# The triangular inverse of an RWKV-7 head kernel: from 128x128 blocks on the whole array to 64x64 blocks in two opposite corners of it

## The chip, the cores and the metric

One core of one Trainium2 chip runs the whole program. The metric is the device time of one execution in microseconds (us). Everything is fp32, or fp32 split into a high and a low part.

## The reference, cut to what matters

Two transformer-like blocks run one after the other on a sequence of 256 tokens of width 1024. The first has an SSD mixer, an attention and a mixture of experts. The second has an RWKV-7 mixer, a convolution and a feed-forward layer. The change touches only the recurrence of the RWKV-7 mixer, which the reference writes token by token for 16 heads of 64 values:

```
sa = einsum('bhvk,bhk->bhv', S, -kk_t)
S  = S * w_t + sa[..., None] * (kk_t * a_t) + v_t[..., None] * k_t
o_t = einsum('bhvk,bhk->bhv', S, r_t)
```

The kernel computes it by blocks of 128 tokens. Within a block the values `sa` depend on each other through a strictly lower triangular 128x128 matrix L, one for each head and token block, and the kernel needs the inverse of I + L. After that, everything is plain products.

## The kernel before, in words

The heads go in 8 pairs (`PAIRS`). A pair has 4 units, 2 heads by 2 blocks of 128 tokens, and `unit(h, t)` numbers them. One step of the loop over pairs interleaves two things on each engine: the inverse of pair p, and the rest of the pair before (`tail`) together with the preparation of the next (`prep`). The order is written out by hand, one function `step` for each engine, in `pe_heads`, `act_heads` and `dve_heads`. Engines hand over by semaphores, and every engine takes its instructions in the written order. Step 0 has no tail, step 7 has no preparation, and `step_loop` runs steps 1 to 6 as a hardware loop of two steps on PE and ACT (DVE writes its own).

The inverse runs by doubling. At level `lev`, `XT` holds the transposed inverses of all diagonal blocks of 2^lev rows and `Xm` the same not transposed. There are seven levels (`LEV`), up to blocks of 128. A level has three parts:

- `below` (line 2269): for each unit, the product of L with the inverse so far, 128x128 by 128x128. The four calls go to two PSUM banks, two units each; such a pair of units is a group g.
- `mask` (L2609, DVE): one instruction for each group keeps the identity and the blocks just under the diagonal, and writes `Ym` (`Xm` at level 0).
- `grow`: for each unit, one product that gives the new half of `Xm` (L2283, not at the last level) and one that gives the new half of `XT` (L2287). Only the 64 columns that change are streamed, picked by the strided view `halves`. ACT copies them back, `Xm` first (L2453) and then `XT` (L2454), one instruction for each group.

Between these, PE works off the tail: `rest` (L2296, L2299), `solve` (L2307), `state` (L2313, L2314) and `outputs` (L2326 to L2328); and the preparation: `decays` (L2224), `turn_ar` and `turn_bk` (transposes) and `grams` (L2252). `grams` contracts over 64 rows only; its calls alternate between the upper and the lower half of the array's rows and write to two different banks.

On DVE, `mask_grams` (L2590) masks the four gram matrices of the next pair. After the second of each two it turns L into I - L (L2599) and writes the level-0 `XT` (L2602). The first half of this stands ahead of the mask of level 6, the second half behind it. The rest of DVE's work of a step, in pieces between the masks, is `differences`, `key_direction`, `state`, `key_and_bonus`, `make_ar`, `make_bk` and `centre` (L2555 to L2630).

In the trace each call of a matmul in fp32 shows as two weight loads and two matmuls; a transpose shows as one of each.

Of the kernel before, what the change touches and what calls it, by code (L numbers as in the profile page):

```python
# [61 lines left out]
def constants():  # L62
# [16 lines left out]
    for lev in range(7):  # L79
        m = 1 << lev  # L80
        pick = ((i[:, None] // m) % 2 == 1) & (i[None, :] // m == i[:, None] // m - 1)
        put(f"level{lev}", np.eye(P) + pick)
        if lev == 0:
            put("level0_t", np.eye(P) + pick.T)
# [100 lines left out]
def build(nc, A, out):  # L185
    ctx = ExitStack()
    with ctx:
# [1982 lines left out]
        Xm, Ym = carve(8960, 4, P), carve(9472, 4, P)  # L2170
# [47 lines left out]
        def pe_heads(pe):  # L2218
# [39 lines left out]
            def below(p, b, lev):  # L2258

                for g in range(2):  # L2260
                    if lev == 0:
                        pe.wait_ge(inverse_begun, 2 * p + g + 1)
                    elif lev == 1:
                        pe.wait_ge(*y_masked.at(2 * LEV * p + g + 1))
                    else:
                        pe.wait_ge(*xm_copied.at(2 * (LEV - 2) * p + 2 * lev + g - 3))
                    for v in range(2):
                        u = 2 * g + v
                        mm = nc.tensor.matmul(bank[g][:, v * P:(v + 1) * P], gram[b][:, u, 0:P],  # L2269
                                              ident if lev == 0 else Xm[:, u, :], start=True, stop=True)  # L2270
                    mm.then_inc(y_made, 1)

            def grow(p, b, lev):

                even, odd = halves(Ym, lev)[0], halves(XT[b], lev)[1]
                for g in range(2):
                    pe.wait_ge(*y_masked.at(2 * LEV * p + 2 * lev + g + 1))
                    if not (isinstance(p, int) and p == 0 and lev == 1):
                        pe.wait_ge(xt_copied, 2 * (LEV - 1) * p + 2 * lev + g - 3)
# [23 lines left out]
            def solve(p, c, t):  # L2303
                pe.wait_ge(xt_copied, 2 * (LEV - 1) * (p + 1))
# [96 lines left out]
            def last():  # L2401
# [16 lines left out]
                pe.wait_ge(xt_copied, 2 * (LEV - 1) * PAIRS)  # L2418
# [7 lines left out]
            step_loop(pe, first, step, last)  # L2426

        def act_heads(act):
# [18 lines left out]
            def grown(p, b, lev):  # L2447
                for g in range(2):
                    r = slice(2 * g, 2 * g + 2)
                    new = bank[2 + g][:, 0:2 * P].rearrange("p (a u n m) -> p a u n m", a=2, u=2, m=1 << lev)  # L2450
                    act.wait_ge(x_made, 2 * (LEV - 1) * p + 2 * lev + g - 1)
                    if lev < LEV - 1:
                        nc.scalar.copy(halves(Xm[:, r, :], lev)[0], new[:, 0]).then_inc(xm_copied.sem, 1)  # L2453
                    nc.scalar.copy(halves(XT[b][:, r, :], lev)[1], new[:, 1]).then_inc(xt_copied, 1)  # L2454
# [9 lines left out]
            def step(p, b, tail=True, prep=True):  # L2464
# [22 lines left out]
                grown(p, b, 5)  # L2487
                grown(p, b, 6)
# [53 lines left out]
        def dve_heads(dve, order):  # L2542
# [44 lines left out]
            def mask_grams(p, c, units):  # L2587
                for u in units:
# [5 lines left out]
                    if u % 2:  # L2594

                        g = slice(u - 1, u + 1)
                        dve.wait_ge(*gram_masked.at(4 * p + u + 1))
                        lt = gram[c][:, g, 0:P]
                        order.step(nc.vector.scalar_tensor_tensor(out=lt, in0=lt, scalar=-1.0,  # L2599
                                                                  in1=ident.unsqueeze(1).to_broadcast([P, 2, P]),  # L2600
                                                                  op0=ALU.mult, op1=ALU.add))
                        nc.vector.tensor_tensor(XT[c][:, g, :], lt, con("level0_t").unsqueeze(1).to_broadcast([P, 2, P]),  # L2602
                                                ALU.mult).then_inc(inverse_begun, 1)

            def mask(p, lev):

                for g in range(2):
                    dve.wait_ge(y_made, 2 * LEV * p + 2 * lev + g + 1)
                    nc.vector.tensor_tensor((Xm if lev == 0 else Ym)[:, 2 * g:2 * g + 2, :],  # L2609
                                            bank[g][:, 0:2 * P].rearrange("p (u s) -> p u s", u=2),  # L2610
                                            con(f"level{lev}").unsqueeze(1).to_broadcast([P, 2, P]),
                                            ALU.mult).then_inc(y_masked.sem, 1)
# [21 lines left out]
            def step(p, b, tail=True, prep=True):  # L2634
# [30 lines left out]
                if prep:  # L2665
                    mask_grams(p + 1, c, (2, 3))

# [31 lines left out]
            def first():  # L2699
                dve.wait_ge(*c_low.at(4))  # L2700
                dve.wait_ge(rk_loaded, 32)
# [8 lines left out]
                mask_grams(0, 0, (2, 3))  # L2710
                gate_convolution(1)
# [288 lines left out]
```

## Time and profile before

| | us |
|---|---|
| median of 3 runs | 1545.48 |
| lowest, highest | 1539.59, 1552.73 |
| profiled execution: its own time | 1549.11 |
| profiled execution: span of the trace | 1547.3 |
| PE busy over the span | 1386.0 (90%) |
| weight loads | 1130.7 (73%) |
| DVE busy | 861.6 (56%) |
| ACT busy | 718.1 (46%) |
| POOL busy | 608.3 (39%) |

PE is TensorE's matmuls, PEld its weight loads, DVE is VectorE, ACT is ScalarE, POOL is GpSimd. A matmul's recorded time is the time it takes to go through the array, and several are under way at once, so a busy share near 100% of PE does not say that it is at its peak; how fast it works is read from the distances between the starts. The page counts the mean granted clock of TensorE over the whole span as 0.938 of full speed. The loop over head pairs occupies the time from about 1064 to 1266 us, in which almost no data is loaded.

### The profile page before, as it was taken

To read this page: it belongs to the slowest core of one execution; us is meant where nothing else is said; L and a number is where in the kernel's file an instruction comes from. 1 tells how busy PE (TensorE), PEld (TensorE's weight loads), DVE (VectorE), ACT (ScalarE), POOL (GpSimd) and SP (SyncE) were. 2 spreads that over 40 slices of the span, in tenths; PEclk is the share of its full clock that TensorE was granted. 3 is DMA by queue.
4 is the path that set the end of the run, shared out by engine and by line. 5 is a ranking of instruction groups with operands and counts; after the bars stand their busy time and mean duration, and the time that the engine had idled before them with its cause. 6 is when DMAs were issued, how large, how long until landed. Compare 5 with 4: busy or idle time off the path is not lost.

```text
span 1547.3 us, 20663 instructions
## 1 busy us (share of the span) xinstructions
PE 1386.0 (90%) x6880; PEld 1130.7 (73%) x6880; DVE 861.6 (56%) x1436; ACT 718.1 (46%) x1209; POOL 608.3 (39%) x324
## 2 busy tenths in 40 slices
PE   5989998788899999997599998859999998799996
PEld 4877876676677777775477776647999986678885
DVE  2283253435688888886413999975666654211112
ACT  4455464434475757665443334443333323344442
POOL 5858658440000000001666565613000005478784
PEclk9989998699999999999899998969999999799999
DMA  6647443038399999993465364612000004355562
GB/s 205 174 118 194 136 134 109 1 109 267 112 354 323 319 310 315 320 317 106 122 196 162 109 190 130 184 42 69 1 0 0 0 11 167 109 163 176 176 190 82
DMA packets 127255, 239.93 MB, mean 155 GB/s; under 512 B 16296, under 2 KB 32346, under 8 KB 127056
## 3 DMA queue, kind: packets, MB, share of 16 engines
q1 hardware_dynamic: 116384, 227.12, 45.9%
q10 hardware_dynamic: 10801, 11.89, 2.7%
q8 instruction: 41, 0.67, 0.2%
q14 instruction: 29, 0.24, 0.0%
HBM read 234.79 MB, written 1.05 MB: 152 GB/s over the span
## 4 chain that ended last, share of the span: by engine, by line
PE 42%; issue 39%; POOL 9%; DVE 7%; ACT 2%; DMA 1%; POOLq 0%; DVEq 0%; ACTq 0%
POOL wlo L291 9%; PE bank L297 7%; PE bank L298 6%; PE bank L299 6%; PE bank L2269 3%; PE bank L2287 3%; PE bank L2283 2%; PE bank L2784 2%; PE bank L2786 2%; PE bank L2785 2%; DVE work L764 2%; PE bank L369 1%; PE bank L2252 1%; DVE work L457 1%; DVE work L998 1%
## 5 line engine op out<-in xcount | busy, mean ns | idle before, releaser
L291 POOL TENSOR_TENSOR wlo<-raw,whi 128x1024 fp32r<-128x1024 f32 (+1 forms) x232 | 565.0, 2454 | 713.8 <-ACT whi L286 713.3
L297 PE MATMUL bank<-whi,t0h 128*128 128x512 f32 (+1 forms) x1072 | 443.1, 413 | 22.0 <-POOL wlo L291 6.7
L286 ACT ACTIVATE whi<-raw 128x1024 fp32r<-128x1024 f32 (+1 forms) x300 | 309.3, 1053 | 280.8 <-PE bank L299 237.7
L298 PE MATMUL bank<-wlo,t0h 128*128 128x512 f32 (+1 forms) x1072 | 431.3, 402 | 0.0
L299 PE MATMUL bank<-whi,t0l 128*128 128x512 f32 (+1 forms) x1072 | 430.9, 402 | 0.0
L297 PEld LDWEIGHTS bank<-whi,t0h 128*128 128x128 f32 x1072 | 208.8, 195 | 79.0 <-issue 23.2
L299 PEld LDWEIGHTS bank<-whi,t0l 128*128 128x128 f32 x1072 | 207.6, 194 | 49.1
L298 PEld LDWEIGHTS bank<-wlo,t0h 128*128 128x128 f32 x1072 | 208.2, 194 | 46.0 <-issue 1.7
L291 DVE TENSOR_TENSOR wlo<-work,whi 128x1024 fp32r<-128x1024 f32 x96 | 113.0, 1218 | 7.5 <-ACT whi L286 7.4
L286 ACT ACTIVATE whi<-work 128x1024 fp32r<-128x1024 f32 x96 | 97.9, 1054 | 5.1 <-PE bank L1459 5.1
L369 PE MATMUL bank<-const,work 128*128 128x128 f32 x128 | 28.8, 419 | 66.4 <-DVE work L457 55.2
L291 DVE TENSOR_TENSOR wlo<-raw,whi 128x1024 fp32r<-128x1024 f32 x68 | 80.2, 1219 | 14.1 <-ACT whi L286 14.1
L2050 DVE SCALAR_TENSOR_TENSOR bank<-work,proj,bank 128x256 f32<-128x256 f32 x203 | 84.8, 483 | 1.9
L2527 POOL TENSOR_TENSOR proj<-proj,small x8 | 5.9, 734 | 194.5 <-PE bank L2328 194.5
L2609 DVE TENSOR_TENSOR work<-bank,const 128x256 f32<-128x256 f32 x112 | 46.6, 423 | 58.3 <-PE bank L2269 54.5
L369 PEld LDWEIGHTS bank<-const,work 128*128 128x128 f32 x128 | 26.1, 226 | 69.5 <-DVE work L457 41.0
L2899 DVE TENSOR_TENSOR t1l<-bank,t1h 128x512 fp32r<-128x512 f32 x16 | 10.3, 686 | 112.3 <-ACT t1h L2856 112.3
L2453 ACT COPY work<-bank 128x128 f32<-128x128 f32 x80 | 21.4, 267 | 82.1 <-PE bank L2287 82.1
L2287 PE MATMUL bank<-work 128*128 128x64 f32 x384 | 57.6, 276 | 1.9 <-DVE work L2609 1.9
L1457 PE MATMUL bank<-whi,t1h 128*128 128x512 f32 x128 | 53.5, 418 | 2.9 <-DVE wlo L291 2.8
L2269 PE MATMUL bank<-work 128*128 128x128 f32 x384 | 55.6, 287 | 0.4 <-DVE work L2609 0.4
L2287 PEld LDWEIGHTS bank<-work 128*128 128x128 f32 x384 | 49.9, 192 | 4.8 <-issue 3.5
(413 smaller groups left out, 2030.0 us busy)
## 6 DMA issues: line engine op xcount, KB each, us to landing
raw<-in_w_ff SPq DMA_DIRECT2D x64, 512.0 KB, 3.6
raw<-in_w_in SPq DMA_DIRECT2D x60, 496.0 KB, 3.6
raw<-in_w_in SPq DMA_DIRECT2D x56, 512.0 KB, 3.6
work<-in_w_exp_down SPq DMA_DIRECT2D x68, 256.0 KB, 5.0
work<-in_w_exp_gate SPq DMA_DIRECT2D x62, 256.0 KB, 5.2
work<-in_w_exp_up SPq DMA_DIRECT2D x62, 256.0 KB, 6.2
raw<-in_w_exp_down SPq DMA_DIRECT2D x60, 256.0 KB, 4.7
raw<-in_w_exp_gate SPq DMA_DIRECT2D x34, 256.0 KB, 5.3
```

Source lines behind the costliest of these rows:

```text
L286: nc.scalar.activation(whi[:, s, 0:width], raw_of(n)[:, 0:width], ACT.Copy).then_inc(hi_ready, 1)
L291: ins = (nc.vector if split_by_vector(n) else nc.gpsimd).tensor_tensor(wlo[:, s, 0:width], raw_of(n)[:, 0:width], whi[:, s, 0:width].bitca ...
L297: nc.tensor.matmul(dst, hi, wh, start=first, stop=False)
L298: nc.tensor.matmul(dst, hi, wl, start=False, stop=False)
L299: return nc.tensor.matmul(dst, lo, wh, start=False, stop=last)
L369: tr = nc.tensor.transpose(bank[4 + b][:, at:at + P], self.src[:, t, (2 * b + kk) * P:(2 * b + kk + 1) * P], ident)
L764: ins = nc.vector.scalar_tensor_tensor(out=convT[:, c, :], in0=xbcT[:, c, w:w + SEQ], scalar=tap, in1=convT[:, c, :], op0=ALU.mult, op1=AL ...
L1457: nc.tensor.matmul(bank[4 + h][:, :], hh, whi[:, s, f], start=first, stop=False, skip_group_check=True)
L2050: ins = nc.vector.scalar_tensor_tensor(out=cvT[:, c, :] if w == W2 - 1 else partial(c), in0=uT[:, c, w:w + SEQ], scalar=tap, in1=partial(c ...
L2269: mm = nc.tensor.matmul(bank[g][:, v * P:(v + 1) * P], gram[b][:, u, 0:P], ident if lev == 0 else Xm[:, u, :], start=True, stop=True)
L2287: mm = nc.tensor.matmul(bank[2 + g][:, P + v * 64:P + (v + 1) * 64], Ym[:, u, :], odd[:, u], start=True, stop=True)
L2609: nc.vector.tensor_tensor((Xm if lev == 0 else Ym)[:, 2 * g:2 * g + 2, :], bank[g][:, 0:2 * P].rearrange("p (u s) -> p u s", u=2), con(f"l ...
```

## The change

- The inverse is made first for the two 64x64 diagonal blocks of each unit, packed above each other: rows 0 to 63 of `XD`, `Xm` and `Ym` belong to the upper block, rows 64 to 127 to the lower. Every product of levels 0 to 5 becomes two calls with 64 rows and 64 columns, one in the upper left corner of the array and one in the lower right, which write to different partitions of the same PSUM bank.
- The growth products stream all 64 columns of a block, and `halves` picks the new ones when ACT copies them.
- Level 6 joins the two blocks: the lower left part of L times the upper inverse (no mask, a plain copy), and that times the lower inverse. ACT copies the two finished diagonal blocks from `XD` into `XT` (`diagonal`), and the quarter of `XT` that stays zero is cleared once at the start.
- `begin_inverse` is taken out of `mask_grams` and stands behind the mask of level 6 and the last gram masks.
- PE's steps 1 to 6 are written out rather than looped. The counts of the semaphores follow.

```diff
-    for lev in range(7):
+    i64 = np.arange(64)
+    for lev in range(6):
...
-        put(f"level{lev}", np.eye(P) + pick)
+        put(f"level{lev}", np.tile(np.eye(64) + pick, (2, 1)))
...
-        Xm, Ym = carve(8960, 4, P), carve(9472, 4, P)
+        Xm, Ym = carve(8960, 4, 64), carve(9472, 4, 64)
+        XD = [carve(9216 + 512 * c, 4, 64) for c in range(2)]
+        XT_COPIES = 2 * (LEV - 1) + 2
+        HALF = [slice(64 * a, 64 * a + 64) for a in range(2)]
...
                     for v in range(2):
                         u = 2 * g + v
-                        mm = nc.tensor.matmul(bank[g][:, v * P:(v + 1) * P], gram[b][:, u, 0:P],
-                                              ident if lev == 0 else Xm[:, u, :], start=True, stop=True)
+                        o = bank[g][:, v * 64:(v + 1) * 64]
+                        if lev == LEV - 1:
+                            mm = nc.tensor.matmul(o[HALF[1]], gram[b][HALF[0], u, 64:P], Xm[HALF[0], u, :], start=True,
+                                                  stop=True)
+                            continue
+                        for r in HALF:
+                            mm = nc.tensor.matmul(o[r], gram[b][r, u, r], ident[r, r] if lev == 0 else Xm[r, u, :],
+                                                  start=True, stop=True)
                     mm.then_inc(y_made, 1)
...
                     if lev < LEV - 1:
                         for v in range(2):
                             u = 2 * g + v
-                            nc.tensor.matmul(bank[2 + g][:, v * 64:(v + 1) * 64], XT[b][:, u, :], even[:, u], start=True,
-                                             stop=True)
-                    for v in range(2):
-                        u = 2 * g + v
-                        mm = nc.tensor.matmul(bank[2 + g][:, P + v * 64:P + (v + 1) * 64], Ym[:, u, :], odd[:, u],
-                                              start=True, stop=True)
+                            for r in HALF:
+                                nc.tensor.matmul(bank[2 + g][r, v * 64:(v + 1) * 64], XD[b][r, u, :], Ym[r, u, :], start=True,
+                                                 stop=True)
+                        for v in range(2):
+                            u = 2 * g + v
+                            for r in HALF:
+                                mm = nc.tensor.matmul(bank[2 + g][r, P + v * 64:P + (v + 1) * 64], Ym[r, u, :],
+                                                      XD[b][r, u, :], start=True, stop=True)
+                    else:
+                        for v in range(2):
+                            u = 2 * g + v
+                            mm = nc.tensor.matmul(bank[2 + g][HALF[0], v * 64:(v + 1) * 64], Ym[HALF[1], u, :],
+                                                  XD[b][HALF[1], u, :], start=True, stop=True)
...
-            step_loop(pe, first, step, last)
+            first()
+            for p in range(1, PAIRS - 1):
+                step(p, p % 2)
+            last()
...
+                        nc.scalar.copy(halves(Xm[:, r, :], lev)[0], halves(new[:, 0], lev)[0]).then_inc(xm_copied.sem, 1)
+                        nc.scalar.copy(halves(XD[b][:, r, :], lev)[1], halves(new[:, 1], lev)[1]).then_inc(xt_copied, 1)
+                    else:
+                        nc.scalar.copy(XT[b][HALF[0], r, 64:P],
+                                       bank[2 + g][HALF[0], 0:P].rearrange("p (u s) -> p u s", u=2)).then_inc(xt_copied, 1)
+
+            def diagonal(p, b):
+                act.wait_ge(xt_copied, XT_COPIES * p + 2 * (LEV - 2))
+                for r in HALF:
+                    nc.scalar.copy(XT[b][r, :, r], XD[b][r, :, :]).then_inc(xt_copied, 1)
...
                 grown(p, b, 5)
+                diagonal(p, b)
                 grown(p, b, 6)
...
+            def begin_inverse(p, c):
+                for u in (1, 3):
...
+                    order.step(nc.vector.scalar_tensor_tensor(out=lt, in0=lt, scalar=-1.0,
+                                                              in1=ident.unsqueeze(1).to_broadcast([P, 2, P]),
+                                                              op0=ALU.mult, op1=ALU.add))
+                    for r in HALF:
+                        nc.vector.tensor_tensor(XD[c][r, g, :], gram[c][r, g, r],
+                                                con("level0_t")[r].unsqueeze(1).to_broadcast([64, 2, 64]),
                                                 ALU.mult).then_inc(inverse_begun, 1)
...
+                    y = bank[g][:, 0:P].rearrange("p (u s) -> p u s", u=2)
+                    if lev == LEV - 1:
+                        ins = nc.vector.tensor_copy(Ym[HALF[1], 2 * g:2 * g + 2, :], y[HALF[1]])
+                    else:
+                        ins = nc.vector.tensor_tensor((Xm if lev == 0 else Ym)[:, 2 * g:2 * g + 2, :], y,
+                                                      con(f"level{lev}").unsqueeze(1).to_broadcast([P, 2, 64]), ALU.mult)
...
                 mask(p, 6)
                 if prep:
                     mask_grams(p + 1, c, (2, 3))
+                    begin_inverse(p + 1, c)
...
             def first():
                 dve.wait_ge(*c_low.at(4))
+                for c in range(2):
+                    order.mark(nc.vector.memset(XT[c][HALF[1], :, 0:64], 0.0))
```

## Rows read from the trace of the kernel before

**Rows 1.** Busy time by stretch: length, each engine's busy time, granted clock, DMA share, GB/s.

```profile
core 0: us, PE busy (x) PEld busy (x) DVE busy (x) ACT busy (x) POOL busy (x), PEclk, DMA share, GB/s
1060.00:1260.00 200.00, 193.95 (x1610) 180.82 (x1609) 127.61 (x306) 62.11 (x237) 14.58 (x16) 1.00 0.01 3
1106.60:1132.20 25.60, 25.09 (x213) 23.64 (x212) 16.75 (x41) 8.00 (x31) 1.43 (x2) 1.00 0.01 2
```

**Rows 2.** Groups by line and shape, 1060 to 1270 us: busy, mean ns, idle before.

```profile
L2287 PE MATMUL bank<-work 128*128 128x64 f32 x384 | 57.6, 276 | 1.9 <-DVE work L2609 1.9
L2269 PE MATMUL bank<-work 128*128 128x128 f32 x384 | 55.6, 287 | 0.4 <-DVE work L2609 0.4
...
L2609 DVE TENSOR_TENSOR work<-bank,const 128x256 f32<-128x256 f32 x112 | 46.6, 423 | 58.3 <-PE bank L2269 54.5 <-DMA raw<-in_ln_x_b 1.6
...
L2453 ACT COPY work<-bank 128x128 f32<-128x128 f32 x80 | 21.4, 267 | 82.1 <-PE bank L2287 82.1
```

**Rows 3.** Timeline of one level inside a step: start, duration, engine, line.

```profile
1119.12 0.53 PEld L2283 LDWEIGHTS bank<-work 128*128 128x128 f32 x4
...
1119.57 0.53 PEld L2287 LDWEIGHTS bank<-work 128*128 128x128 f32 x4
...
1120.52 0.61 PE L2287 MATMUL bank<-work 128*128 128x64 f32 x4
...
1121.16 0.27 ACT L2453 COPY work<-bank 128x128 f32<-128x128 f32 x1 [0.46 <-PE bank L2287]
...
1121.58 0.97 PEld L2269 LDWEIGHTS bank<-work 128*128 128x128 f32 x8
1121.63 1.11 PE L2269 MATMUL bank<-work 128*128 128x128 f32 x8
...
1122.33 0.87 DVE L2609 TENSOR_TENSOR work<-bank,const 128x256 f32<-128x256 f32 x2 [1.47 <-PE bank L2269]
1122.47 0.53 PEld L2307 LDWEIGHTS bank<-work 128*128 128x128 f32 x4
```

**Rows 4.** Timeline of the end of that step, from the last growth to the next level 0.

```profile
1131.68 0.53 PEld L2287 LDWEIGHTS bank<-work 128*128 128x128 f32 x4
...
1132.27 0.73 PEld L2252 LDWEIGHTS bank<-work 64*128 64x128 f32 x8
1132.28 1.13 PE L2252 MATMUL bank<-work 64*128 64x256 f32 x8
...
1133.34 0.97 PEld L2269 LDWEIGHTS bank<-work 128*128 128x128 f32 x8 [0.33 <-issue]
...
1133.44 1.29 DVE L2590 TENSOR_TENSOR work<-bank,const 128x512 f32<-128x512 f32 x2 [0.66 <-PE bank L2252]
1134.76 0.42 DVE L2599 SCALAR_TENSOR_TENSOR work<-work,const 128x256 f32<-128x256 f32 x1
1134.78 0.73 PEld L2252 LDWEIGHTS bank<-work 64*128 64x128 f32 x8 [0.47 <-DVE work L2590]
...
1135.56 0.75 DVE L2609 TENSOR_TENSOR work<-bank,const 128x256 f32<-128x256 f32 x2
...
1137.54 0.42 DVE L2599 SCALAR_TENSOR_TENSOR work<-work,const 128x256 f32<-128x256 f32 x1
...
1138.00 0.42 DVE L2602 TENSOR_TENSOR work<-work,const 128x256 f32<-128x256 f32 x1
...
1138.85 0.87 DVE L2609 TENSOR_TENSOR work<-bank,const 128x256 f32<-128x256 f32 x2 [0.43 <-PE bank L2269]
```

**Rows 5.** Timeline, the same place one step later.

```profile
1157.92 0.49 PE L2252 MATMUL bank<-work 64*128 64x256 f32 x2
```

**Rows 6.** Weight loads by shape, whole trace.

```profile
L2283 PEld LDWEIGHTS bank<-work 128*128 128x128 f32 x320 | 42.2, 192 | 1.3 <-DVE work L2609 0.7 <-issue 0.5
...
L1891 PEld LDWEIGHTS bank<-proj,work 128*64 128x64 f32 x32 | 4.3, 137 | 2.7 <-issue 0.4
```

**Rows 7.** DVE and ACT instructions of other sizes, 1060 to 1270 us.

```profile
L2590 DVE TENSOR_TENSOR work<-bank,const 128x512 f32<-128x512 f32 x28 | 17.9, 682 | 6.7 <-PE bank L2252 6.7
...
L2441 ACT COPY work<-bank 128x512 f32<-128x512 f32 x7 | 4.1, 586 | 0.1
...
L2432 ACT ACTIVATE work<-bank 128x256 f32<-128x256 f32 x7 | 2.7, 383 | 6.6 <-PE bank L2224 6.6
```

**Rows 8.** Busy time by stretch, in the attention, where the clock was low.

```profile
254.50:268.00 13.50, 11.79 (x57) 10.43 (x57) 4.22 (x14) 5.39 (x18) 10.21 (x25) 0.51 0.06 23
```

More of the change, by code:

```diff
@@ L78, in constants @@
     put("amask", np.concatenate([neg, np.zeros((P, P)), neg], axis=1))
[L79 removed]
+    i64 = np.arange(64)
+    for lev in range(6):
         m = 1 << lev
[L81 to L82 removed]
+        pick = ((i64[:, None] // m) % 2 == 1) & (i64[None, :] // m == i64[:, None] // m - 1)
+        put(f"level{lev}", np.tile(np.eye(64) + pick, (2, 1)))
         if lev == 0:
[L84 removed]
+            put("level0_t", np.tile(np.eye(64) + pick.T, (2, 1)))
     put("heads", (i[:, None] // 64 == i[None, :] // 64) * 1.0)
@@ L2449, in grown @@
                     r = slice(2 * g, 2 * g + 2)
-                    new = bank[2 + g][:, 0:2 * P].rearrange("p (a u n m) -> p a u n m", a=2, u=2, m=1 << lev)
                     act.wait_ge(x_made, 2 * (LEV - 1) * p + 2 * lev + g - 1)
                     if lev < LEV - 1:
-                        nc.scalar.copy(halves(Xm[:, r, :], lev)[0], new[:, 0]).then_inc(xm_copied.sem, 1)
-                    nc.scalar.copy(halves(XT[b][:, r, :], lev)[1], new[:, 1]).then_inc(xt_copied, 1)
+                        new = bank[2 + g][:, 0:2 * P].rearrange("p (a u s) -> p a u s", a=2, u=2)
+                        nc.scalar.copy(halves(Xm[:, r, :], lev)[0], halves(new[:, 0], lev)[0]).then_inc(xm_copied.sem, 1)
[7 more added lines that the diff above has]
+                    nc.scalar.copy(XT[b][r, :, r], XD[b][r, :, :]).then_inc(xt_copied, 1)
             def copy_rest(p, t):
@@ L2593, in mask_grams @@
                                                 [P, 2, 2 * P]), ALU.mult).then_inc(gram_masked.sem, 1)
[L2594 to L2602, printed above, removed]
+            def begin_inverse(p, c):
+                for u in (1, 3):
+                    g = slice(u - 1, u + 1)
+                    dve.wait_ge(*gram_masked.at(4 * p + u + 1))
+                    lt = gram[c][:, g, 0:P]
+                    order.step(nc.vector.scalar_tensor_tensor(out=lt, in0=lt, scalar=-1.0,
[4 more added lines that the diff above has]
+                                                con("level0_t")[r].unsqueeze(1).to_broadcast([64, 2, 64]),
                                                 ALU.mult).then_inc(inverse_begun, 1)
@@ L2608, in mask @@
                     dve.wait_ge(y_made, 2 * LEV * p + 2 * lev + g + 1)
[L2609 to L2612, printed above, removed]
+                    y = bank[g][:, 0:P].rearrange("p (u s) -> p u s", u=2)
[4 more added lines that the diff above has]
+                                                      con(f"level{lev}").unsqueeze(1).to_broadcast([P, 2, 64]), ALU.mult)
+                    ins.then_inc(y_masked.sem, 1)
             def state(p):
@@ L2710, in first @@
                 mask_grams(0, 0, (2, 3))
+                begin_inverse(0, 0)
                 gate_convolution(1)
```

9 lines of the change are left out of this document (4 added, 5 removed).

## The prediction

> **What bounds the kernel now.** I read the busy times by stretch first. Over the loop of head pairs, PE is busy 193.95 of 200 us at full granted clock, DVE 127.61, ACT 62.11, and the DMA share is 0.01 [rows 1]. So no transfer is waited for here, and what the loop saves comes off the total one to one: nothing is loaded in it that could be late behind it. The view of groups by line says who waits for whom. The masks wait 54.5 us for PE's `below`, and the copies of the new half wait 82.1 us for PE's `grow`, while the idle time of PE before the same lines is 1.9 and 0.4 us [rows 2]. PE is the bound and the others wait for it.
>
> The timeline of one level says what PE is bound by. The two calls of L2283 take 0.45 us from their first load to the next line's (1119.12 to 1119.57). The four calls of L2269, with twice as many columns streamed, take 0.89 us (1121.58 to 1122.47) [rows 3]. That is 0.2225 us for a call in both cases, 64 columns or 128: the weight load sets the pace, not the stream. The step repeats after 25.65 us (1132.28 to 1157.92, less 0.01 of rounding) [rows 4, 5]. I split it into the stretch from the first mask of level 0 to the first gram product, 1138.85 to 1157.92 = 19.07 us, and the end of the step, 1132.27 to 1138.85 = 6.58 us [rows 4, 5].
>
> **The change part by part.**
>
> **Cost of a corner call.** A weight load of 64 columns lasts 137 ns where one of 128 lasts 192 [rows 6], 55 ns less, which is half of the 111 ns (0.2225/2) that a load takes up at full pace. The stream of 64 columns needs no more than that. So a corner call takes some 0.0565 us x 2 = 0.113 us; I take 0.116. Do the two corners work at once? The nearest row is L2252: 4 calls of 256 columns each, in the upper and lower row halves by turns, need 1.07 us to the next line's load [rows 4]. At the 0.2225 us for 128 columns of L2269, four calls of 256 columns one after another would take 4 x 0.445 = 1.78 us. So the row halves do run side by side there. I take this for the corners too: 0.116 us for a pair. The bounds are 0.116 (side by side) and 0.232 (in turn) for a pair.
>
> **PE's calls.** Before, a step has 7 x 4 calls of `below` and 5 x 8 + 4 of `grow` = 72, at 0.2225 = 16.0 us. After, there are 6 x 8 + 4 = 52 and 5 x 16 + 4 = 84, 136 in all: 64 pairs and 8 single calls of level 6 = 72 slots at 0.116 = 8.35 us. Gain 7.7 us a step on PE alone.
>
> **Switching.** Before L2252 its load comes 0.59 us after the first load of the four records of L2287, which need 0.445 (1131.68 to 1132.27), so 0.145 us is lost; behind it 1.07 us pass where two pairs need at most 2 x 0.445 = 0.89, so some 0.2 us is lost (0.18 at least), and the load shows 0.33 idle put down to issue [rows 4]. Going between whole-array calls and tiled calls empties the array. The tail and the preparation stay whole-array calls and stand between nearly all parts of the inverse: in at `below` 0, 1, 3, 5 and `grow` 1 to 5, out again as often, 18 new switches a step at 0.145 to 0.2 = 3.1 us. The ends are nothing (if the array stood waiting anyway) and 0.33 each = 5.9 us.
>
> **The long stretch, 19.07 us.** It holds `below` and `grow` 1 to 5, 60 of the calls: 13.35 us become 60 x 0.116 = 6.96, that is -6.4; 16 of the switches add 2.8. PE now also waits where it was covered: behind `below` 0 it needs the mask, behind `grow` the copy of `Xm`, which comes 0.3 us after the last matmul (1120.52 + 0.33 to 1121.16) and takes 0.27, now 64 elements instead of 128, 0.21 by the slope between 128 and 512 elements (267 and 586 ns) [rows 2, 3, 7]. While `grow` of group 1 lasts 0.46 this is 0.1 to 0.2 short at `below` where no filler stands between, hence about 0.3 us over the stretch beside what the switches hide. The sum is -6.4 + 2.8 - 0.3 (the shorter masks) = -3.9: 15.15 us.
>
> **The masks** take 128 elements where they took 256: 424 ns less 128 x 1.0 ns (the slope from 256 to 512 elements, 423 to 682) = 0.30 us [rows 2, 7]; 12 of these and 2 plain copies of the same size. That is 14 x 0.13 = 1.8 us less of DVE's 16.75 us in 25.6 [rows 1]. `begin_inverse` gives 0.35 back (two products of 0.3 for one of 0.42, twice). DVE then has 15.3 us of work; with 0.04 us between neighbours (0.46 from start to start for 0.42, 1137.54 to 1138.00 [rows 4]) for 45 instructions and 1.2 us for one gram product waited for, 18.3: not the bound at 22, but the floor under any better outcome.
>
> **The end of the step, 6.58 us.** Ahead of mask 6 fall the L2599 and L2602 of the first group (0.88 us, 1134.76 to mask 6 at 1135.56, overlapped) [rows 4]. `gram_masked` is unchanged, so the second grams still wait for the first masks: load at +0.05, masks 1.17 us later at the earliest, as 1132.27 to 1133.44; two of 0.65 each; then STT 0.46 and two halves 0.5 until `below` 0 may start, and DVE is busy with the second group for another 0.95 until it takes mask 0. From the first gram product: 1.17 + 1.3 + 1.2 (grams and their latency, with mask 6 inside) + 1.3 + 0.95 + 0.95 = 6.9. The end is 0.3 longer: what moves away ahead of mask 6 is paid at the end, twice over, since `below` 0 of group 0 can no longer begin earlier. `grow` 6, the next `rest` and `decays` lie beside this on PE.
>
> **ACT.** `diagonal` adds two copies of 256 elements, 0.38 each [rows 7]. They stand ahead of the level-6 copies, which wait for mask 6 and the second grams; ACT is 31% busy. I cost them at nothing; if PE's `solve` came to wait for them, 0.77 us a step. The two clears at the start (0.3 each at most, 128x256 masks take 0.42) stand ahead of DVE's first `differences`: 0.7 us at most, which I count. No DMA and no queue of SP or POOL is passed; POOL waits for `outputs` only.
>
> **Sum.** A full step goes from 25.65 to 15.15 + 6.9 = 22.05, -3.6; six of these make -21.6. Step 0, without a tail, has only 4 switches (0.7), but its levels cannot go below the round trip matmul, mask, matmul, copy, about 1.9 us (0.56 + 0.33 + 0.77 + 0.23, from slots, masks and the 0.3 us that a consumer starts late) against 1.39 of calls: 5 levels leave 6.4 - 0.7 - 2.0 = -3.7. Step 7 has 72 calls and the tail's switches, 7.7 - 2.5 - 0.7 = -4.5. With +0.7 for the clears: -29 us. The profiled execution took 1549.1 us, 3.6 above the median of the runs; it goes to 1520, and the median from 1545.5 to 1516.
>
> **The rivals.**
>
> **The corners take turns (slower).** Both corners write to the same PSUM bank, which no pair of row halves in this trace does: `grams` alternates its banks. If the bank admits one of them at a time, the 136 calls cost 136 x 0.116 = 15.8 us, 0.2 less than now, and the switches (3.1) and the end (0.3) come on top: +3.2 us a step, +26 in 8, 1571. The decision lies at 0.165 us a pair: (16.0 - 3.4 - 0.8)/72, with 0.8 for waits. Against it: the corners lie in different partitions, so no output column is shared. The Trainium skill (TensorEngine Tiling, section Gotcha 1: PSUM Pressure) says that different row tiles cannot access the same PSUM bank simultaneously; taken by the letter that is this rival, and no run here shows it yet.
>
> **Dearer switches, or longer waits between levels.** With 0.25 to 0.3 us a switch (the 0.33 above), 18 x 0.1 = 1.8 us more a step: -1.8 x 8 = -14 and 1531. For it: switches into and out of a corner are new, and no row has them.
>
> **The clock falls.** It is granted in full all through the loop, with PE busy 97% [rows 1]. In the attention it stood at 0.51, that is nearly always at 1.2 of 2.4 GHz, with PE busy 11.79 of 13.5 us, at short calls with waits between [rows 8]. After the change PE has 8.35 + 7.9 us of calls in 22 us (7.9 is 25.65 less 16.0 and some 1.7 of waits, 0.47 + 0.33 + 0.43 and smaller ones [rows 4]). If a quarter of the loop ran at half clock, the 16.3 us of calls would last 4 us more in each step and the gain would be gone: 1547.
>
> **More than forecast.** With free switches (-2.8 a step) and waits down to near DVE's floor of 18.3: 19.2 us a step, -6.4 x 8 = -51 and 1494.
>
> **How the numbers follow.** Forecast 0.64 (1498 to 1526), dearer switches 0.13, corners in turn 0.16, the clock 0.04, more than forecast 0.03. The range leaves out most of the corners in turn and a bit below: 1494 to 1562, which holds 0.82. About 1%, or 15 us, is what a measurement of this kernel can tell from no change. Faster by more than that is below 1530: the forecast, the better case, and a little under half of the dearer switches, 0.68 (the forecast's own tail, 0.04, taken off). That tail, the rest of the dearer switches and the clock make 0.16 within 1%, and the corners in turn 0.16 slower.
>
> **What would show it.** Right: the `below` and `grow` groups of two calls a corner start 0.23 and 0.46 us apart from the next; matmuls of the two corners start within some 10 ns of each other; loads near 137 ns; each change to a tail line shows about 0.2 us between matmul and load; the step repeats after some 22 us; masks of 0.3 us; granted clock 1.00. Wrong: corner matmuls at even distances of 0.058 us (in turn), a step above 25.65, masks that no longer wait for PE at all (DVE bound), a PEclk below 0.95 in the loop, or the step's end, first gram to mask 0, much above 6.9.

## The result, and the profile after

| | before | after |
|---|---|---|
| median of 14 runs each, us | 1544.05 | 1531.93 |
| lowest, highest | 1539.59, 1559.53 | 1526.62, 1542.36 |
| profiled execution, its span | 1549.11, 1547.3 | 1526.62, 1524.8 |

The ratio is 0.9923 with a 95% interval of 0.9897 to 0.9950. The kernel is 12 us faster where 29 were forecast; 1531.9 lies inside the stated range of 1494 to 1562. The profiled execution happens to be the fastest of its 14.

The step of the loop repeats from one first gram product (L2256) to the next. These rows of the timeline after (start, duration, engine, line) show three such products, at 1118.75, 1143.86 and 1166.18. Behind the second stands the end of a step, with its second grams (1146.46), up to mask 0 (L2644):

```profile
1118.75 1.14 PE L2256 MATMUL bank<-work 64*128 64x256 f32 x8
...
1143.86 1.13 PE L2256 MATMUL bank<-work 64*128 64x256 f32 x8
...
1146.46 1.13 PE L2256 MATMUL bank<-work 64*128 64x256 f32 x8 [0.86 <-DVE work L2618]
...
1148.80 0.42 DVE L2628 SCALAR_TENSOR_TENSOR work<-work,const 128x256 f32<-128x256 f32 x1
...
1150.35 0.61 DVE L2632 TENSOR_TENSOR work<-work,const 64x128 f32<-64x128 f32 x2
1150.99 0.29 DVE L2644 TENSOR_TENSOR work<-bank,const 128x128 f32<-128x128 f32 x1
1151.01 0.45 PE L2279 MATMUL bank<-const,work 64*64 64x64 f32 x8 [0.65 <-DVE work L2632]
...
1166.18 1.14 PE L2256 MATMUL bank<-work 64*128 64x256 f32 x8
```

The step from 1143.86 takes 22.32 us, 7.13 to mask 0 and 15.19 from there to the next first gram product. Before it was 25.65, 6.58 and 19.07 [rows 4, 5]. But the step before it, 1118.75 to 1143.86, takes 25.11, and the six steps 1 to 6 take 25.14, 22.32, 25.11, 22.32, 23.84 and 23.83 us. The view of busy times by stretch says why. Its columns are those of [rows 1]; the stretches are, by turns, the end of a step (7.1 us) and the rest of it:

```profile
1071.30:1078.40 7.10, 5.23 (x52) 3.87 (x48) 4.99 (x12) 2.45 (x9) 0.00 (x0) 1.00 0.00 0
1078.40:1096.40 18.00, 17.93 (x292) 16.22 (x292) 9.48 (x30) 5.34 (x24) 1.34 (x2) 0.81 0.01 2
1096.40:1103.50 7.10, 5.26 (x52) 3.88 (x48) 5.72 (x14) 2.46 (x10) 0.00 (x0) 1.00 0.01 3
1103.50:1118.70 15.20, 15.09 (x292) 13.52 (x292) 9.45 (x31) 5.32 (x24) 1.34 (x2) 1.00 0.01 2
1118.70:1125.80 7.10, 5.28 (x53) 3.88 (x48) 5.72 (x14) 2.48 (x10) 0.00 (x0) 1.00 0.01 2
1125.80:1143.80 18.00, 17.88 (x292) 16.17 (x292) 9.50 (x31) 5.31 (x24) 1.34 (x2) 0.81 0.01 2
...
1126.60:1133.40 6.80, 6.80 (x79) 6.25 (x77) 3.16 (x11) 1.35 (x6) 0.00 (x0) 0.50 0.00 0
```

Both kinds of step hold the same 292 matmul records in their long part. Where the clock is granted in full they take 15.2 us; where its mean is 0.81, 18.0. In the stretch that begins at 1126.6 it stands at 0.50, at 1.2 of 2.4 GHz. Ahead of each fall lies an end of step in which PE is busy only 5.2 to 5.3 of 7.1 us. The same holds of the ends that no fall follows (5.26 us from 1096.40), so a thin end alone does not decide it. Before the change the clock was 1.00 throughout the loop [rows 1].

The corners themselves work as hoped. These rows of the timeline are `below` 6 (L2275), four calls in one corner; `below` 3 (L2279), eight calls in two corners; `solve` (L2323), two calls on the whole array; and parts of `grow` 3 (L2293, L2298), four calls a line in two corners:

```profile
1144.93 0.67 PE L2275 MATMUL bank<-work 64*64 64x64 f32 x8
...
1157.95 0.68 PE L2279 MATMUL bank<-work 64*64 64x64 f32 x16
1158.56 0.66 PE L2323 MATMUL bank<-work 128*128 128x64 f32 x4
1159.15 0.45 PE L2293 MATMUL bank<-work 64*64 64x64 f32 x8
1159.43 0.40 PE L2298 MATMUL bank<-work 64*64 64x64 f32 x8
1159.66 0.40 PE L2293 MATMUL bank<-work 64*64 64x64 f32 x8
```

Eight calls in two corners take 0.68 us, as four in one do (0.67), and a line of four calls takes 0.23 us (1159.43 to 1159.66): 0.115 us a pair. The rows also price the switches. Eight corner calls need 4 x 0.115 = 0.46 us and `solve` starts 0.61 behind their start, so 0.15 is lost; the two calls of `solve` need 0.445 and the next corner call starts 0.59 behind theirs, so 0.145 is lost. A weight load of a corner lasts 142 ns in the mean, where one of the whole array lasted 192 [rows 6]:

```profile
L2298 PEld LDWEIGHTS bank<-work 64*64 64x64 f32 x640 | 26.7, 142 | 0.0
```

A second loss lies ahead of the loop. In the timeline after, DVE, POOL and PE in the prelude:

```profile
1054.13 2.74 DVE L2632 TENSOR_TENSOR work<-work,const 64x128 f32<-64x128 f32 x2
1054.38 2.34 POOL L292 TENSOR_TENSOR wlo<-raw,whi 128x1024 fp32r<-128x1024 f32 x1 [1.66 <-ACT whi L287]
1056.90 1.29 DVE L2732 TENSOR_TENSOR proj<-proj,bank 128x512 f32<-128x512 f32 x2
1058.24 1.16 PE L2228 MATMUL bank<-proj,const 128*128 128x128 f32 x4 [5.09 <-DVE proj L2732]
```

The last two instructions of `begin_inverse` (L2632), 0.60 or 0.61 us elsewhere, take 2.74 us here. They end at 1056.87, just behind POOL's making of the low part of a weight tile ("POOL's split" below), which is over at 1056.72. The gate of the convolution (L2732) stands behind them on DVE, and PE waits 5.09 us for it. Before the change the same wait was 1.55 us:

```profile
1063.11 0.71 PE L2224 MATMUL bank<-proj,const 128*128 128x128 f32 x4 [1.55 <-DVE proj L2697]
```

The third loss lies behind the loop. These are the stretches from the last first gram product to the first product of the next stage, before and after:

```profile
1234.88:1272.85 37.97, 35.06 (x273) 31.29 (x273) 21.23 (x46) 10.71 (x41) 3.28 (x4) 1.00 0.01 1
1213.85:1253.50 39.65, 33.93 (x404) 28.31 (x401) 20.55 (x50) 11.19 (x45) 3.54 (x4) 0.87 0.01 2
```

This stretch, step 7 and the tail of the last pair, has become 1.7 us longer, with the clock at half for 10.2 us of it.

### The profile page after: what moved, and what is told of

Read it like the earlier page. It is cut to its first block and busy times, and to the rows that moved or that the text cites. A ratio compares the mean times of both kernels' runs of the same rounds, so it can differ in the third digit from the quotient of the medians.

```text
span 1524.8 us, 22521 instructions
## 1 busy us (share of the span) xinstructions
PE 1351.3 (89%) x7904; PEld 1086.8 (71%) x7904; DVE 848.3 (56%) x1454; ACT 717.0 (47%) x1225; POOL 612.0 (40%) x324
## 5 line engine op out<-in xcount | busy, mean ns | idle before, releaser
L292 DVE TENSOR_TENSOR wlo<-raw,whi 128x1024 fp32r<-128x1024 f32 x68 | 80.3, 1221 | 13.9 <-ACT whi L287 13.9
L1458 PE MATMUL bank<-whi,t1h 128*128 128x512 f32 x128 | 53.9, 421 | 2.8 <-DVE wlo L292 2.8
L2644 DVE TENSOR_TENSOR work<-bank,const 128x128 f32<-128x128 f32 x96 | 27.0, 292 | 49.4 <-PE bank L2279 47.8
L2822 PE MATMUL bank<-whi,t1h 128*128 128x512 f32 x128 | 50.7, 396 | 2.1 <-DVE t1l L2937 2.1
L1460 PE MATMUL bank<-whi,t1l 128*128 128x512 f32 x128 | 51.2, 400 | 0.0
L1459 PE MATMUL bank<-wlo,t1h 128*128 128x512 f32 x128 | 51.0, 398 | 0.0
L2824 PE MATMUL bank<-whi,t1l 128*128 128x512 f32 x128 | 50.6, 395 | 0.0
```

Source lines behind the costliest of these rows:

```text
L292: ins = (nc.vector if split_by_vector(n) else nc.gpsimd).tensor_tensor(wlo[:, s, 0:width], raw_of(n)[:, 0:width], whi[:, s, 0:width].bitca ...
L1458: nc.tensor.matmul(bank[4 + h][:, :], hh, whi[:, s, f], start=first, stop=False, skip_group_check=True)
L1459: nc.tensor.matmul(bank[4 + h][:, :], hh, wlo[:, s, f], start=False, stop=False, skip_group_check=True)
L1460: mm = nc.tensor.matmul(bank[4 + h][:, :], hl, whi[:, s, f], start=False, stop=last, skip_group_check=True)
L2822: nc.tensor.matmul(o, t1h[:, c, r], whi[:, s, f], start=False, stop=False, skip_group_check=True)
L2824: mm = nc.tensor.matmul(o, t1l[:, c, r], whi[:, s, f], start=False, stop=last, skip_group_check=True)
```

## The experiments

In what follows, "step" is the time from one first gram product to the next, "prelude" that from the very first one to mask 0 of step 0 (11.30 us before, 15.19 after).

**Filler that keeps PE at work.** Filler is matmul calls whose results are never read: here three small ones a step, put where PE waits for DVE. `busy` is set in steps 1 to 6; the two calls behind `below` 6 stand in step 0 as well, and step 7 has none.

```diff
+            def keep_busy(b, calls, cols=256):
+                for _ in range(calls):
+                    nc.tensor.matmul(bank[b][HALF[1], 256:256 + cols], ident[HALF[1], HALF[1]], con("amask")[HALF[1], 0:cols],
+                                     start=True, stop=True)
...
+                    if busy and g:
+                        keep_busy(1, 1)
...
+                    keep_busy(2, 2)
                     grams(p + 1, c, (2, 3))
```

> The changed kernel, with three calls of filler in each of steps 1 to 6: one corner, 64 rows by 64 columns by 256 streamed, results never read. Two stand where PE waits for the first gram masks (behind `below` 6), one between the two groups of `below` 0, where PE waits for the second half of `begin_inverse`. Theory (the clock): in the changed kernel the loop's steps take 22.32 us while the clock is granted in full and 23.8 to 25.1 us where it is granted in half for 3.4 or 6.8 us, and it falls in the thin stretch from the first grams to level 1. The filler fits into waits of 0.86 and 0.65 us, so it costs at most 0.5 us a step itself. With it the granted clock of the loop is 1.00, all six steps take 22.3 to 22.8 us and the kernel is 6 to 9 us faster than the changed kernel (ratio to before about 0.987). Rival (the long steps are long for another reason, such as instruction fetch of the loop that is written out, and the clock falls because PE waits): the long steps stay at 24 to 25 us with the clock full, and the time is the changed kernel's or up to 3 us more.

All six steps take 22.32 us, 133.91 together against 142.55. The ratio is 0.9877 (0.9849 to 0.9904), the median 1524.42 us, 7.5 less than the changed kernel's. The busy times of the same stretches as above, the six steps as one at the end:

```profile
1092.40:1099.50 7.10, 6.36 (x58) 4.26 (x54) 5.72 (x14) 2.46 (x9) 0.00 (x0) 1.00 0.01 3
1099.50:1114.70 15.20, 15.11 (x292) 13.52 (x292) 9.44 (x31) 5.34 (x24) 1.34 (x2) 1.00 0.01 2
...
1070.09:1204.00 133.91, 128.91 (x2080) 106.67 (x2077) 90.32 (x257) 46.86 (x198) 8.07 (x12) 1.00 0.01 2
```

PE does more work in the end of the step, 6.36 us instead of 5.26, the rest is as it was, and the clock stays at 1.00. The theory holds, and the fetch of the written-out loop, which is still there, is ruled out as the cause of the long steps. In step 7, which has no filler in its `below` 0, the clock falls for 6.8 us where it had fallen for 3.4, and the stretch behind the loop takes 41.07 us instead of 39.65. This fits that of the 8.6 us won in the loop only 7.5 show in the medians.

**The changed kernel again.**

> The changed kernel as it is, beside the combination, so that the two are compared on one chip. Theory (the clock falls by chance of phase, in the thin stretch from the first grams to level 1): the steps again fall into 22.3 us where the clock is full and 23.8 or 25.1 us where it is half for a while, in another pattern than in the first profile; the time is 1528 to 1536 us. Rival (a fixed cause in some steps): the same steps as in the first profile are long.

1532.43 us, ratio 0.9902 (0.9874 to 0.9930). The steps are 25.11, 22.31, 25.10, 22.32, 23.83 and 23.83 us: the same ones are long. So my theory of a chance phase was wrong in this form: the falls came at the same places in both traces of this kernel. The next run shows that the place is not fixed by the step's own code.

**The first inverse begun behind the gate.**

```diff
-                begin_inverse(0, 0)
                 gate_convolution(1)
+                begin_inverse(0, 0)
```

> The changed kernel, with the first inverse begun behind `gate_convolution(1)` in `first` rather than ahead of it. Theory (DVE is held up by POOL in the prelude): in the changed kernel two half instructions of `begin_inverse` take 2.74 us there, until POOL's split of 2.34 us ends, and PE waits 5.1 us for the gate behind them, against 1.55 us before the change. With the gate first, the stretch from the first gram product to mask 0 of step 0 falls from 15.2 to about 12 us and the kernel gains 3 us (ratio to before about 0.990). Rival (the gate itself would then be held up by the same split, or `below` 0 waits for the inverse instead): the stretch stays within 1 us of 15.2 and no time is gained.

The prelude is 13.65 us, a gain of 1.5, half of what was expected. PE now waits 1.38 us for the gate, but the halves meet the next split and last 2.63 us, and `below` 0 waits for them:

```profile
1060.72 2.63 POOL L292 TENSOR_TENSOR wlo<-raw,whi 128x1024 fp32r<-128x1024 f32 x1 [1.67 <-ACT whi L287]
...
1061.18 2.63 DVE L2632 TENSOR_TENSOR work<-work,const 64x128 f32<-64x128 f32 x2
...
1063.87 0.45 PE L2279 MATMUL bank<-const,work 64*64 64x64 f32 x8 [2.29 <-DVE work L2632]
```

So theory and rival were both half right: the gate was held up, and the inverse is held up too. Prelude and step 0 together take 25.65 us instead of 26.34, only 0.7 less; the clock is at half for 3.4 us of this step 0. The loop's code is unchanged here, and yet its long steps are others: 22.31, 25.14, 23.78, 22.31, 25.11 and 22.32 us. So where the falls come depends on what ran ahead of the loop. The ratio, 0.9893 (0.9866 to 0.9920), can't tell 1.5 us.

**The first half of the inverse begun ahead of mask 6 again** (in the loop only).

```diff
                     mask_grams(p + 1, c, (0, 1))
+                    begin_inverse(p + 1, c, (1,))
                 mask(p, 6)
                 if prep:
                     mask_grams(p + 1, c, (2, 3))
-                    begin_inverse(p + 1, c)
+                    begin_inverse(p + 1, c, (3,))
```

> The changed kernel, with the first half of `begin_inverse` of the loop's steps moved back to where it stood before the change, ahead of mask 6; the second half stays behind. Theory (the new place is not a gain): behind mask 6 DVE waits 0.75 us for the second grams, which the first half (1.05 us) would fill, so mask 6 is later by 1.05, the gram masks by 0.3 and mask 0 earlier by 0.7 us a step: 21.6 us a step at full clock instead of 22.3, some 4 us in all, a little more if the shorter wait also keeps the clock up. Rival (mask 6 counts: its delay reaches `grow` 6, `rest` and `solve`): steps of 22.3 us or more, no gain or a loss of up to 1 us a step.

Steps at full clock take 21.95 us, 0.37 less (0.7 was expected), with 6.60 us from gram product to mask 0 instead of 7.12. One step, with the clock low in it, took 25.51. Behind the loop the clock is at half for 13.7 us in one piece. Ratio 0.9891 (0.9861 to 0.9922). The new place costs 0.37 us a step.

**Calls ordered by corner.** In `below` and `grow` the loop over the two corners stands outside that over the two units:

```diff
-                    for v in range(2):
-                        for r in HALF:
+                    for r in HALF:
+                        for v in range(2):
```

> The changed kernel, with the calls of levels 0 to 5 ordered by corner, both units of the upper corner first and then both of the lower, instead of alternating; the same calls, the same banks, the same data. Theory (the gain comes from two corners at work at once, and calls of one corner follow each other): a group of two and two takes three slots instead of two, so 12 groups of `below` and 10 groups of two products in `grow` take 32 slots of 0.116 us more, 3.7 us a step, 22.3 becoming 25 to 26 us at full clock and the kernel 20 to 28 us slower than the changed one, slower than before by some 10 us (ratio 1.005). Rival (the array takes loads and matmuls of all four calls side by side whatever their order, or the weight loads alone set the pace): steps of 22.3 us, no change.

Steps at full clock are 22.70 us, only 0.38 more. The rival was nearer: the halves of the array need no alternation in the program, a line of four calls still takes 0.23 to 0.24 us:

```profile
1197.98 0.45 PE L2300 MATMUL bank<-work 64*64 64x64 f32 x8
1198.21 0.45 PE L2295 MATMUL bank<-work 64*64 64x64 f32 x8
1198.45 0.45 PE L2300 MATMUL bank<-work 64*64 64x64 f32 x8
```

Which call runs beside which the records do not say, since they do not name the corner. Ratio 0.9927 (0.9896 to 0.9958).

**The kernel before, PE's loop written out.** `step_loop(pe, first, step, last)` replaced by `first()`, `for p in range(1, PAIRS - 1): step(p, p % 2)`, `last()`.

> The kernel before, with PE's steps 1 to 6 written out instead of looped and nothing else changed. Theory (the written-out loop is worth nothing): the loop's end cost no time before, since all its steps take 25.65 us, so the steps are 25.65 us again. Rival (register arithmetic or the loop's end is paid on PE): 25.0 to 25.5 us a step. A second rival (fetching longer code costs): above 25.7.

All six steps take 25.62 us (25.65 before): writing the loop out is worth 0.2 us in all. One run, 1545.27 us.

**The kernel before, with the move alone.**

```diff
                 mask(p, 6)
                 if prep:
                     mask_grams(p + 1, c, (2, 3))
+                    begin_inverse(p + 1, c)
```

with the same taken out of `mask_grams`, and `begin_inverse(0, 0)` behind the gram masks in `first`.

> The kernel before, with only the move: the start of the next inverse (both halves, still 128x128) behind mask 6 and the last gram masks, in the loop and in `first`. Theory (the move gains nothing by itself and costs a little): mask 6 comes 0.88 us earlier, but the second gram masks wait for PE's product all the same, and two halves of 0.9 us then stand ahead of mask 0: the end of the step goes from 6.58 to 6.8 to 7.3 us and the step from 25.65 to 25.9 to 26.4; in the prelude the gate is held up as in the changed kernel, some 3 us. Rival (mask 6 is on the path of `grow` 6, and the next step begins earlier): steps of 25.4 us or less.

Five steps take 25.68, one 25.75: the move is worth nothing there, and its cost is below what I expected. With the corners it cost 0.37 a step. The prelude is 12.73 us, 1.4 longer than before; of the moved instructions only the first is long (1.61 us), the other three take 0.42 or 0.43. So the move alone explains 1.4 of the 3.9 us that the prelude grew in the changed kernel; the pair of 2.74 us has no like here. One run, 1547.85 us.

**The three mends together:** filler, first half early in the loop, and in `first` each half behind its own gram masks again.

```diff
                 mask_grams(0, 0, (0, 1))
+                begin_inverse(0, 0, (1,))
                 mask_grams(0, 0, (2, 3))
-                begin_inverse(0, 0)
+                begin_inverse(0, 0, (3,))
                 gate_convolution(1)
```

> The changed kernel with three edits together: the three filler calls a step that kept the clock up, the first half of `begin_inverse` ahead of mask 6 in the loop's steps, and in `first` the two halves each behind their own gram masks with the gate behind both, as in the kernel before. Theory (the three costs are separate and add up): the loop's steps take 21.95 us each at full clock, 131.7 us for six against 142.5 in the changed kernel; the stretch from the first gram product to mask 0 falls from 15.2 to about 11.6 us; together 11 + 3.5 = 14 us less than the changed kernel, near 1518 us, ratio to before 0.983. Rival (the clock falls again, since the filler behind `below` 6 now lies in a shorter wait, and in the prelude DVE is held by POOL's split wherever the halves stand): steps of 22 to 24.5 us, the stretch above 13 us, and the time that of the filler alone, 1524.

The median is 1517.16 us beside 1532.43 of the changed kernel on the same chip, the ratio 0.9793 (0.9765 to 0.9820). Steps are 21.94 or 21.95 us, the prelude 11.43, prelude and step 0 together 23.13 (26.34 in the changed kernel). With the six steps that is 14.1 us less, as the theory had it. The six steps in one stretch:

```profile
1076.17:1207.83 131.66, 127.66 (x2080) 107.93 (x2076) 90.79 (x257) 46.76 (x198) 8.04 (x12) 1.00 0.01 2
```

**The same without the filler.**

> The combination without the filler calls. Theory (the clock): without them it falls in the loop again, in the thin stretch at the head of some steps; one to four of the six steps take 23.4 to 25.5 us where the others take 21.95, and the kernel is 3 to 8 us slower than the combination, 1520 to 1525 us. Rival (with the first half early the thin stretch is short enough): all six steps at 21.95, time as the combination's.

1523.75 us, ratio 0.9852 (0.9821 to 0.9883), 8.3 us above the kernel that follows here (1515.43), which ran on the same chip and has one more edit, worth 0.4 us in its trace. As the theory had it, the clock falls in the loop again. Five steps are 21.94 or 21.95 us, one is 25.58, and in that one the clock is low:

```profile
1070.18:1114.06 43.88, 40.83 (x684) 34.81 (x680) 29.79 (x85) 15.59 (x66) 2.67 (x4) 1.00 0.01 2
1114.06:1121.40 7.34, 6.07 (x58) 4.71 (x56) 5.80 (x14) 2.25 (x9) 0.00 (x0) 0.84 0.01 2
1121.40:1139.64 18.24, 18.22 (x292) 16.42 (x288) 9.51 (x30) 5.55 (x26) 1.34 (x2) 0.78 0.01 2
1139.64:1205.47 65.83, 61.21 (x1024) 52.19 (x1020) 45.80 (x130) 23.39 (x99) 4.03 (x6) 1.00 0.01 2
```

In the profiled execution that is 3.6 us. Another 2.6 lie behind the loop, from the last first gram product to the next stage, where the clock is at half for 13.7 us instead of 6.8. The stretch without the filler, and the same in the three mends together:

```profile
1205.47:1245.57 40.10, 34.97 (x404) 29.08 (x401) 20.93 (x51) 11.17 (x45) 3.53 (x4) 0.83 0.01 2
1207.83:1245.37 37.54, 33.10 (x408) 27.17 (x405) 20.57 (x50) 11.17 (x45) 3.53 (x4) 0.91 0.01 2
```

So the filler in the loop also changes where the clock falls behind it, and most of the 8.3 us is found.

**Step 7: the scaling of the heads earlier.** On the combination: `scale_heads(0)` behind mask 2 instead of mask 4, `head_roots(0)` behind `grown` 1 instead of 3.

> The combination of the three edits, with `scale_heads(0)` of step 7 behind mask 2 rather than mask 4 (and the roots it needs behind ACT's growth copies of level 1). Theory (step 7 is bound by DVE from mask 4 on): in the combination DVE works without a gap from 1224.96 to 1232.65 us, 2.8 us of it `scale_heads`, and mask 6 comes last, while it waits 1.43, 2.56 and 1.67 us between masks 2, 3 and 4. Filling these waits brings mask 6 of step 7 from 25.0 us behind the last preparation's first gram product to 22.5 to 23.5, and the kernel gains 1.5 to 2.5 us. Rival (the masks between are on the path, and the 2.8 us only move): mask 6 at 25 us or later, no gain.

Mask 6 of step 7 comes 24.42 us behind the last preparation's first gram product, against 24.82. The ratio is 0.9795 (0.9764 to 0.9826), the combination's. The theory was wrong. In the timeline of DVE, mask 5 now waits for PE, and what stands between masks 5 and 6 is `centre` and the gate, which did not move:

```profile
1218.73 0.29 DVE L2652 TENSOR_TENSOR work<-bank,const 128x128 f32<-128x128 f32 x1 [2.34 <-PE bank L2286]
...
1221.31 1.22 DVE L2731 TENSOR_TENSOR proj<-proj 128x1024 f32<-128x1024 f32 x1
1222.56 1.29 DVE L2735 TENSOR_TENSOR proj<-proj,bank 128x512 f32<-128x512 f32 x2
1223.88 0.50 DVE L2650 COPY work<-bank 64x128 f32<-64x128 f32 x2
```

**Filler in step 7 too:** `keep_busy(2, 2)` also where `prep` is false.

> The kernel with `scale_heads(0)` early, and the two filler calls behind `below` 6 in step 7 as well, where PE waits for mask 6 behind the gating of the heads. Theory (the clock): in the combination it is half for 3.4 us twice behind this place (1234.5 and 1241.4); keeping PE at work brings 1 to 2 us. Rival (the stretch behind, with 0.5 to 1 us of waiting at each short product, is thin enough by itself): the same low stretches, no gain.

Ratio 0.9798 (0.9768 to 0.9828), and both stretches of low clock are still there behind mask 6. The rival holds; nothing is gained.

## Why the prediction was wrong, point by point

**What bounds the kernel:** right for the kernel before. No transfer showed up behind the shorter loop (its DMA share is still 0.01).

**The corner call, 0.116 us a pair:** right, 0.115. The corners write to one bank at once: eight calls in two corners take 0.68 us, like four in one. The rival of corners in turn, which I gave 0.16 and 1571 us, is disproved. The rule of the Trainium skill (TensorEngine Tiling, Gotcha 1: PSUM Pressure), that different row tiles cannot access the same PSUM bank simultaneously, does not hold for these two tiles, which write to different partitions of the bank; here the measurement decides.

**Switching and the two stretches:** right. The long stretch was to be 15.15 us and is 15.19; the end 6.9 and is 7.12 or 7.13; the step 22.05, and is 22.32 at full clock. A switch cost 0.145 to 0.15 us each way, so dearer switches did not happen. Part of the agreement is luck: the working of the long stretch names 0.3 us of new waits and leaves them out of its sum, which would be about 15.45 with them. That the median lies in the stated range, and beside the 1531 of the dearer switches, is luck too: the range was widened for two rivals of which neither happened.

**The clock is the step that failed.** The sum took the full clock of the loop before as given, and so put the cost of a fall at nothing; as a rival it had a chance of 0.04. PE's own work fell, by my sum, from 24 to 16.3 us a step, and the thinnest part, where PE waits for DVE at the end of the step, was priced in time only. In the profiled execution it cost 142.55 - 133.91 = 8.6 us, and the filler gave back 7.5 us of the medians. The price I had given a fall was rather high: 4 us a step for a quarter of the loop at half clock makes 2.3 for the seventh of it that was at half (1 - 0.93, doubled), and it was 1.4. I had written the sign for it, a PEclk below 0.95 in the loop; it is 0.93:

```profile
1071.30:1213.85 142.55, 130.85 (x2045) 112.56 (x2041) 90.57 (x257) 46.82 (x198) 8.06 (x12) 0.93 0.01 2
```

**The prelude:** I priced two clears at 0.7 us and the move of `begin_inverse` in `first` at nothing. Prelude and step 0 were to bring -3.0 us. The prelude grew by 3.9 (11.30 to 15.19), step 0 shrank by 5.2 (16.32 to 11.15): -1.3. (The clears take 0.55 us far ahead of the first gram product, and DVE waits for a transfer behind them. Step 0's -3.7 had a slip as well: five levels at 1.9 instead of 1.39 us take back 2.5 us and not 2.0.) What I missed is that DVE's gate stood behind the moved halves, and that POOL's splits hold such halves up. I had read POOL's queue only for its order.

**Step 7:** -4.5 was forecast. The stretch from the last first gram product to the next stage became 1.7 us longer (37.97 to 39.65). Up to mask 6 it is 1.1 shorter, 26.93 us instead of 28.04. The clock was at half for 3.4 us there; with the three mends it was not, and mask 6 came after 24.82 us, 0.6 of the difference by the earlier first half (6.53 us to mask 0 instead of 7.12). DVE works without a gap from the scaling of the heads to mask 6, 8.0 us before (1254.92 to 1262.92) and 7.7 after (1233.09 to 1240.78), which PE's shorter calls don't touch; I had not looked at DVE there. Behind mask 6 the stretch is 2.8 us longer, 12.7 instead of 9.9, with the clock at half for 6.8 us of it. The runs settle what this is. With 3.4, 6.8, 10.2 and 13.7 us at half clock the stretch takes 11.2 (corner order), 12.7, 13.9 (first inverse behind the gate) and 15.3 us (no filler), 1.4 us for each 3.4, and by this line some 9.8 at full clock (an estimate), as before. So the clock took about 2.8 us there and about 1.5 ahead of mask 6, and at full clock step 7 and the tail would have gained some 2.6 (estimates).

**The sum:** six steps -11.4 (forecast -21.6: 1.6 by the step at full clock, 8.6 by the clock), prelude and step 0 -1.3 (-3.0), step 7 and the last tail +1.7 (-4.5; some -2.6 without the clock): -11.0 us where -29 was forecast, beside -12.1 of the medians. The rest of the profiled executions differs where nothing was changed, so that is scatter. Behind the heads it is 274.5 us before and 271.3 after, but 274.8 in the second trace of the changed kernel, and 271.9 to 275.6 in the other runs. Ahead of the first gram product it is 1053.35 and 1044.96 us, and between 1043.6 and 1053.0 in the others, with changed kernels at both ends and the old one written out at 1050.3.

## What to carry to other kernels

A faster engine is not only idle longer: where TensorE's granted clock hangs on its work, as here, time saved by making its calls smaller can be lost to half clock behind the thinnest part of a loop. Price the loop at both clock levels, and try a few calls of unread filler in waits that are there anyway. Look also at the clock behind the loop, where it can fall in place of it. Before a difference of two profiles is put down to a change, look at the stretches that the change did not touch: here they differed by 3.2 and 8.4 us. An instruction moved on an in-order engine delays all that stands behind it, in the prelude as in the loop, and there beside whatever other engine works at that time.

## What the runs showed of the hardware

- Two 64x64 tiles in opposite corners of TensorE, with outputs in different halves of one PSUM bank, run side by side at 0.115 us a pair (fp32, 64 columns). Ordered by corner instead of by turns they cost 0.38 us more a step (22.70 against 22.32).
- A switch between whole-array and corner calls loses 0.145 to 0.15 us each way beside the calls' own pace (1157.95 to 1159.15), as one from whole-array calls to row halves did before (0.145 [rows 4]).
- Three small filler calls a step (6.36 instead of 5.26 us busy of 7.1) held the clock at 1.00 for 134 us. The falls without them came at the same steps in two traces of one kernel, and at others when only the prelude was changed.
- DVE instructions on SBUF alone lasted longer beside POOL's split: 2.74 and 2.63 us for two that take 0.6, and 1.61 for one L2628 of 0.42. They ended 0.15, 0.46 and 0.28 us behind the end of the split. That the split holds them up is read from these times; no run took the split away.
